# A transformer kernel on one core: the first attention's index branch is projected first, its scores and choice of keys lie between the later projections

## What is computed

```python
mod = c_act @ w_ada[layer] + b_ada[layer]          # 6 x 1024 modulation values
u = modulate(rmsnorm(h, attn_gain[layer]), a_shift, a_scale)
q, k, v, iq, ik, iw = split(u @ w_in)              # 1024, 256, 256, 512, 64, 8 columns
q, k, iq, ik = apply_rope(each)
iw = iw * (IDX_HEADS ** -0.5 * IDX_DIM ** -0.5)
rel = relu(einsum('bqhd,bsd->bqhs', iq, ik))       # 8 index heads, one index key
# index = sum over heads of iw * rel, causal; the 64 best keys of each query are kept
s = einsum(q, k) * HEAD_DIM ** -0.5                # 16 heads, 4 key heads
p = masked_softmax(s, chosen keys)
h = h + a_gate * ((p @ v) @ w_out)
```

## Time and profile before

| | us |
|---|---|
| median of three runs | 2263.2 |
| lowest, highest | 2262.22, 2263.34 |
| span of the profiled execution, first to last instruction | 2254.8 |
| projections, from the first to the last (span time) | 47.06 to 122.07 |
| index scores and choice of keys | 124.76 to 149.34 |
| attention, up to the output projection | 149.34 to 184.00 |
| first feed-forward matmul | 227.46 |

### The profile page before, as it was taken

How to read it: one execution, slowest core, us unless ns; L and a number is a source line. 1 busy time by engine, 2 the same in 40 slices (tenths; PEclk the granted TensorE clock), 3 DMA queues, 4 the chain that set the end, 5 groups by cost and what they waited for, 6 DMA issues and landing times.

```text
span 2254.8 us, 75616 instructions
## 1 busy us (share of the span) xinstructions
PE 2072.8 (92%) x34420; PEld 1800.9 (80%) x34420; DVE 613.6 (27%) x1472; ACT 409.8 (18%) x820; POOL 11.8 (1%) x20
## 2 busy tenths in 40 slices
PE   5967999999999999999999999999988977899998
PEld 3846888878657899999898989898977666777776
DVE  2577553331453201010101010101025372322222
ACT  2033000020463101111111111111112422211111
POOL 0000000000010000000000000000000000000000
PEclk8979999999899899999999999999999998899999
DMA  9453978653475599999999999999981101399996
GB/s 353 146 187 111 374 281 317 241 187 116 152 270 196 194 395 335 393 342 390 385 396 390 396 389 396 387 396 389 396 326 38 38 1 37 156 405 403 405 399 262
DMA packets 253308, 640.84 MB, mean 284 GB/s; under 512 B 15152, under 2 KB 21424, under 8 KB 247984
## 3 DMA queue, kind: packets, MB, share of 16 engines
q1 hardware_dynamic: 252384, 634.93, 74.9%
q10 hardware_dynamic: 848, 4.84, 0.6%
HBM read 638.68 MB, written 1.05 MB: 284 GB/s over the span
## 4 chain that ended last, share of the span: by engine, by line
PE 68%; DMA 20%; DVE 6%; ACT 2%; SPq 2%; issue 1%; DVEq 0%; POOLq 0%; POOL 0%; ACTq 0%
PE psum L745 22%; DMA ring<-in_moe_w_up 13%; PE psum L503 9%; DMA ring<-in_w_up 6%; PE psum L645 3%; PE psum L654 3%; PE psum L630 3%; PE psum L848 3%; PE psum L725 2%; SPq L2275 2%; PE psum L1084 1%; PE psum L839 1%; PE psum L1234 1%; PE psum L798 1%; PE psum L463 1%; PE psum L513 1%
## 5 line engine op out<-in xcount | busy, mean ns | idle before, releaser
L745 PE MATMUL psum<-uT,ring 128*64 128x80 f32 (+1 forms) x14336 | 564.5, 237 | 24.1 <-DMA ring<-in_moe_w_up 21.8
L745 PEld LDWEIGHTS psum<-uT,ring 128*64 128x64 f32 x14336 | 532.5, 137 | 54.2 <-DMA ring<-in_moe_w_up 37.6
L745 PE MATMUL psum<-arena,ring 128*64 128x80 f32 (+1 forms) x7168 | 269.4, 236 | 0.0
L745 PEld LDWEIGHTS psum<-arena,ring 128*64 128x64 f32 x7168 | 263.8, 137 | 0.0
L1755 DVE TENSOR_TENSOR arena<-arena,psum 128x288 f32<-128x288 f32 x56 | 25.4, 454 | 730.6 <-PE psum L745 730.6
L1385 ACT ACTIVATE arena<-psum 128x384 f32<-128x384 f32 x56 | 27.4, 490 | 697.9 <-PE psum L745 697.9
L1608 DVE SCALAR_TENSOR_TENSOR arena<-ring,cact,arena 128x512 f32<-128x512 f32 x168 | 126.3, 752 | 6.0
L503 PE MATMUL psum<-uT,ring 128*128 128x256 f32 (+1 forms) x496 | 111.0, 384 | 3.6 <-ACT uT L1290 3.6
L503 PEld LDWEIGHTS psum<-uT,ring 128*128 128x128 f32 (+1 forms) x496 | 94.2, 191 | 22.0 <-issue 8.3
L503 PE MATMUL psum<-arena,ring 128*128 128x256 f32 x384 | 86.2, 386 | 4.9 <-ACT arena L1290 3.6
L645 PE MATMUL psum<-uT,ring 128*128 128x256 f32 x352 | 80.1, 387 | 10.4 <-DMA ring<-in_ffn_w_gate 10.4
(11 more groups left out here) (417 smaller groups left out, 2081.2 us busy)
## 6 DMA issues: line engine op xcount, KB each, us to landing
ring<-in_moe_w_gate SPq DMA_DIRECT2D x224, 512.0 KB, 11.1
ring<-in_moe_w_up SPq DMA_DIRECT2D x224, 512.0 KB, 10.1
ring<-in_moe_w_down SPq DMA_DIRECT2D x224, 512.0 KB, 11.1
ring<-in_w_ada SPq DMA_DIRECT2D x36, 2048.0 KB, 14.3
ring<-in_w_up SPq DMA_DIRECT2D x19, 2048.0 KB, 11.2
ring<-in_w_down SPq DMA_DIRECT2D x19, 2048.0 KB, 9.9
ring<-in_w_gate SPq DMA_DIRECT2D x19, 2048.0 KB, 10.5
ring<-in_ffn_w_gate SPq DMA_DIRECT2D x5, 2048.0 KB, 7.8
```

The costliest lines, as they stand in the source:

```text
L745: mm = pe.matmul(out(HD * hc), w[:, c0 + HD * hc:c0 + HD * hc + HD], x, skip_group_check=True, **kw)
```

## The change

The index branch comes first. Chunks are loaded in the order `win.3`, `win.4`, `win.0`, `ada0.4`, `ada0.5`, `win.1`, `win.2`, `ada0.6`. The 16 index scores are split into groups of four, six and six behind the query projections, their relus and sums likewise, and the two choices of keys lie between the sums and the rotary steps on VectorE. Keys and v are projected last. The weighing of `ada0.6` is cut into its eight blocks, one behind the maximum of each attention unit, and the column sums of `ada0.4` to `ada0.6` go into the attention on TensorE. The arithmetic is the same.

```diff
-        for n, (c0, c1) in enumerate(((0, 512), (512, 1024), (1024, 1536), (1536, 2048), (2048, 2120))):
-            add_cols(f"win.{n}", w_in, c0, c1)
-        for c in range(FIRST, 7):
+        def add_win(n):
+            add_cols(f"win.{n}", w_in, 512 * n, min(512 * n + 512, w_in.shape[1]))
+        add_win(3)
+        add_win(4)
+        add_win(0)
+        for c in range(FIRST, 6):
             add_cols(f"ada0.{c}", A["w_ada"][0], 512 * c, 512 * c + 512)
+        add_win(1)
+        add_win(2)
+        add_cols("ada0.6", A["w_ada"][0], 512 * 6, 512 * 6 + 512)
...
+            def index_scores(i0, i1):
+                pe.wait_ge(s_rope, 3)
+                for i in range(i0, i1):
+                    t, h = i // IDX_H, i % IDX_H
+                    L, r = P * (t + 1), (h % 2) * HD
+                    b, _ = open_job(pe, "I", "A")
+                    pe.matmul(b[:, 0:L], iqT[r:r + HD, h // 2, P * t:P * t + P], ikd[r:r + HD, 0:L],
+                              start=True, stop=True).then_inc(res, 1)
+            w = chunk("win.3")
             proj("raw", "A", w, 0, 2, uT, base=0)
             proj("raw", "A", w, 256, 2, uT)
+            frees("win.3")
+            rope_unit("pair", 0)
+            w = chunk("win.4")
+            proj("raw", "A", w, 0, 1, uT, rows=HD)
+            rope_unit("pair", 1)
+            tokproj("iw", "V", w, 64, 8, uT)
+            frees("win.4")
+            w = chunk("win.0")
+            proj("raw", "A", w, 0, 2, uT)
+            rope_unit("one", 2)
+            proj("raw", "A", w, 256, 2, uT)
             frees("win.0")
-            rope_unit("pair", 0)
+            rope_unit("pair", 3)
+            index_scores(0, 4)
             w = chunk("win.1")
             proj("raw", "A", w, 0, 2, uT)
-            rope_unit("pair", 1)
+            rope_unit("pair", 4)
+            index_scores(4, 10)
             proj("raw", "A", w, 256, 2, uT)
             frees("win.1")
-            rope_unit("pair", 2)
+            rope_unit("pair", 5)
+            index_scores(10, 16)
             w = chunk("win.2")
             proj("raw", "A", w, 0, 2, uT)
-            rope_unit("pair", 3)
+            rope_unit("pair", 6)
+            rope_unit("dup", 7)
             tokproj("v", "A", w, 256, 256, uT)
...
+            def first_sums(s):
+                if s in (2, 3):
+                    column_sums(s - 1, acc0(s + 2), 4 * (s + 2))
+                if s == len(att_units("dsa")):
+                    column_sums(3, acc0(6), 24)
...
             attention("dsa", [lambda r, g, L: kd[r:r + HD, 0, g, 0:L]],
-                      [lambda w, j, g: vt[0:w, 0, j, HD * g:HD * g + HD]])
+                      [lambda w, j, g: vt[0:w, 0, j, HD * g:HD * g + HD]], first_sums)
...
+            raws(0)
+            raws(1)
+            raws(2, rows=HD, n=1)
+            raws(3)
+            raws(4)
+            index_relu(0, 4)
+            raws(5)
+            index_relu(4, 10)
+            raws(6)
+            index_relu(10, 16)
+            raws(7)
+            copy_job("v", vt[:, 0], lambda b: b3(b, 2))
             attention("dsa")
...
                     if s < len(units):
                         scored(s)
+                    if kind == "dsa" and s < KT:
+                        weigh_block("ada0.6", acc0(6), s)
                     if s >= 2:
                         combine(s - 2)
...
+            V(rope_pair(iqT[:, 0:2, :], raw[:, 0], mark["raw"][0]), s_rope)
+            weigh("ada0.4", acc0(4))
+            V(rope_pair(iqT[:, 2:4, :], raw[:, 1], mark["raw"][1]), s_rope)
+            b = next_job(dve, "iw", "V")
+            V(ts(iw[:], b[:, 0:16].rearrange("p (t n) -> p t n", t=2), IDX_H ** -0.5 * HD ** -0.5, None, ALU.mult), dve_took)
+            weigh("ada0.5", acc0(5))
+            V(rope_dup(b3(ikd, 1), ("dup0", "rotdup0"), 1), s_rope)
+            V(rope_pair(qT[:, 0:2, :], raw[:, 1], mark["raw"][3]), s_rope)
+            index_sums(0, 4)
+            V(rope_pair(qT[:, 2:4, :], raw[:, 0], mark["raw"][4]), s_rope)
+            index_sums(4, 8)
+            best_keys(0)
+            index_sums(8, 10)
+            V(rope_pair(qT[:, 4:6, :], raw[:, 1], mark["raw"][5]), s_rope)
+            index_sums(10, 16)
+            best_keys(1)
+            V(rope_pair(qT[:, 6:8, :], raw[:, 0], mark["raw"][6]), s_rope)
+            V(rope_dup(kd[:, 0, 0:2, :]))
+            V(rope_dup(kd[:, 0, 2:4, :]), s_rope)
             attention("dsa", [selm])
```

More of the change, by code:

```diff
@@ L891, in _ @@
             mm.then_inc(res, 1)
-            w = chunk("win.0")
+            def index_scores(i0, i1):
[6 more added lines that the diff above has]
+                              start=True, stop=True).then_inc(res, 1)
@@ L905, in _ @@
             proj("raw", "A", w, 0, 2, uT)
-            rope_unit("pair", 3)
+            rope_unit("pair", 6)
+            rope_unit("dup", 7)
             tokproj("v", "A", w, 256, 256, uT)
             frees("win.2")
[L909 to L923, removed]
-            pe.wait_ge(s_rope, 8)
[L925 to L931, removed]
+            def first_sums(s):
[3 more added lines that the diff above has]
+                    column_sums(3, acc0(6), 24)
@@ L1419, in _, with index_relu @@
             act.activation(trig[:], ang[:, 0:2, :], ACT.Sin).then_inc(s_trig, 1)
[L1420 to L1428, removed]
+            def index_relu(i0, i1):
+                for i in range(i0, i1):
+                    L = P * (i // IDX_H + 1)
                     b = next_job(act, "I", "A")
-                    i = IDX_H * t + h
                     if i >= 2:
@@ L1599, in mods_from, with weigh_block @@
                 V(stt(m, o, float(D), bias.rearrange("p (a b) -> p a b", b=1).to_broadcast([P, w // rep, rep]), ALU.mult, ALU.add), s_mod)
-            def weigh(name, acc):
[L1603 to L1608, removed]
+            def weigh_block(name, acc, k):
+                slot, val, a, b = place[name]
+                w = slot_view(slot, a, b)
+                if k == 0:
+                    dve.wait_ge(land[slot], val)
+                    V(ts(acc, w[:, 0, :], cact[:, 0:1], None, ALU.mult))
+                else:
+                    V(stt(acc, w[:, k, :], cact[:, k:k + 1], acc, ALU.mult, ALU.add), s_acc if k == KT - 1 else None)
+            def weigh(name, acc):
+                for k in range(KT):
+                    weigh_block(name, acc, k)
             def gain(dst, scale, g):
@@ L1937, in _, with index_sums @@
             dve.wait_ge(s_trig, 1)
-            for i in range(4):
-                V(rope_pair(qT[:, 2 * i:2 * i + 2, :], raw[:, i % 2], mark["raw"][i]), s_rope)
-                if i % 2:
-                    weigh(f"ada0.{4 + i // 2}", acc0(4 + i // 2))
-            V(rope_dup(kd[:, 0, 0:2, :]))
-            V(rope_dup(kd[:, 0, 2:4, :]), s_rope)
-            weigh("ada0.6", acc0(6))
-            V(rope_pair(iqT[:, 0:2, :], raw[:, 1], mark["raw"][5]), s_rope)
-            V(rope_pair(iqT[:, 2:4, :], raw[:, 0], mark["raw"][6]), s_rope)
-            b = next_job(dve, "iw", "V")
-            V(ts(iw[:], b[:, 0:16].rearrange("p (t n) -> p t n", t=2), IDX_H ** -0.5 * HD ** -0.5, None, ALU.mult), dve_took)
-            V(rope_dup(b3(ikd, 1), ("dup0", "rotdup0"), 1), s_rope)
             causal = pk("causal", NT)
-            for t in range(NT):
-                L = P * (t + 1)
-                for h in range(IDX_H):
-                    i = IDX_H * t + h
+            def index_sums(i0, i1):
+                for i in range(i0, i1):
+                    t, h = i // IDX_H, i % IDX_H
+                    L = P * (t + 1)
                     dve.wait_ge(*mark["I"][i])
@@ L1961, in _, with best_keys @@
                         V(stt(acc8[:, 0:L], rel[:, i % 2, 0:L], w, acc8[:, 0:L], ALU.mult, ALU.add), s_relused)
+            def best_keys(t):
+                L = P * (t + 1)
                 V(tt(work[:, 0:L], acc8[:, 0:L], causal[:, t, 0:L], ALU.add))
```

## The result

| | before | changed |
|---|---|---|
| median (range) of 4 runs each, us | 2262.71 (2261.66 to 2263.34) | 2246.75 (2244.59 to 2251.13) |
| ratio, 95% interval | | 0.9933 [0.992, 0.9945] |
| span of the profiled execution, us | 2254.8 | 2244.6 |
| first masked score, us from the span's start | 149.34 | 135.88 |
| output projection, us | 184.00 | 170.18 |

The account below looks back on a forecast made before the run. It took the choice of keys, exposed with TensorE nearly unused, as what to hide; −17.9 + 1.2 + 1.7 + 1.0 = −14.0 gave a span of 2240.8 us and a time of 2249.2 us, range 2244.8 to 2253.6.

Parts of the forecast that it names:

- The bound: Ahead of attention, the choice of keys costs 24.5 us with TensorE nearly unused.
- The walk: New order stepped through up to attention: first masked score at 131.5 instead of 149.34, 17.9 us earlier.
- The rule that what stands ahead in an engine's list is finished first: On VectorE, the 9.1 us choice ahead of the last query pair's rotary holds v back.
- The alternative without that rule: VectorE free to take the last rotary first: v would start at 120.5, the sum would be −16.5.
- The clock behind iw, +1.7: Wide projection behind iw's narrow matmuls: 3.4 us at half speed, 1.7 us lost.
- The clock in v, +1.0: Low clock in v after TensorE's 2.5 us wait: 1.0 us lost, taken between 0 and 1.7.
- Attention, +1.2: Third weighing's eight blocks in attention overfill VectorE's waits: 1.2 us lost, bounds 0 and 6.0.
- Behind it: From the output projection on, order is unaltered and all moves as one piece; first feed-forward matmul stays 43.5 us behind.
- (a): Rival: TensorE is never held and the clock never falls; −19.2, 2244.0 us; chance 0.15.
- (b): Rival: index scores wait for ScalarE's relus and the clock is low in attention; −9.9, 2253.3 us; chance 0.18.
- (c): Rival: the clock stays down after the narrow matmuls, through the projections; +7.9, 2271.1 us; chance 0.02.
- (d): Rival: bank rotation keeps the order from being realised, choice of keys exposed again; gain about 0, 2263 us; chance 0.03.

Follow-up runs that it names:

- scores_last: Changed kernel with all index scores, relus, sums and both choices of keys put back behind v: 2262.3 us, ratio 0.9995 to the kernel before.
- choice_last: Changed kernel with the second choice of keys moved behind the last rotary steps on VectorE: 2250.16 us, ratio 0.9948 to the kernel before.
- iw_merged: Changed kernel with iw computed as eight more rows of the index key's projection, turned back by two small transposes: 2240.18 us, ratio 0.9902 to before.
- split_choice: Changed kernel with the last rotary steps put between four and four rounds of the second choice of keys: 2246.38 us, ratio 0.9926 to before.
- weighed_early: Changed kernel with ada0.6 weighed whole in VectorE's wait behind the index key's rotary, not in attention blocks: 2249.89 us, ratio 0.9945 to before.
- changed_again: The changed kernel itself, unaltered, timed and profiled again beside later variants: 2249.54 us, ratio 0.994 to the kernel before.
- split_and_merged: Changed kernel with the edits of both split_choice and iw_merged: 2236.96 us, ratio 0.9881 to the kernel before.
- filled_wait: Changed kernel with two more matmuls of 512 columns, whose result nobody reads, ahead of v: 2250.12 us, ratio 0.9945 to before.

## Why the prediction was right, point by point

- **The bound.** Right. The exposed choice of keys went beside the projections, and with it the gain comes and goes (scores_last).
- **The walk.** Right to half a us. It gave 98.1 us for the rotation of the second query pair including the clock (96.4 + 1.7), and VectorE took it up at 98.39. The waits came out near what was written: 1.8 foretold at the index scores and 1.61 measured, though the releaser is VectorE's rotary step behind the first choice and not ScalarE's relu; 7.04 and 5.26 us left to VectorE ahead of the projections, where 6 and 5 were foretold. v was to start at 123.0 + 1.7 = 124.7 and did at 124.94, after a wait of 2.19 (2.5 foretold).
- **The rule that what stands ahead in an engine's list is finished first.** It holds for both sides: the choice held the rotary and v (changed), and the rotary's wait held the choice (choice_last). The alternative without that rule, v at 120.5, is out.
- **The clock behind iw, +1.7.** Right: 8.41 us on the chain where the clean projections took 6.91, 1.5 lost. The fall itself came at 71.2, in the last us of iw's matmuls, and lasted to 74.6.
- **The clock in v, +1.0.** Too small, and the first step that was off. I took a value between 0 and 1.7, which was a choice and not worked out; v took 8.88, which is 1.97 over 6.91. Of this 1.7 is the clock, the upper bound (8.86 and 7.17 for v behind the same wait in iw_merged). The rest is that 6.91 is the spacing of projections that follow each other without a wait; behind a wait v takes 7.2 even at full clock. With the 0.24 us by which v starts later, v ends 1.2 us behind the forecast (133.82 and 132.6). Another 0.46 us went missing between v's end and the first masked score: 2.06 us, where the walk had 1.6 (129.9 to 131.5). The walk counted the copy and the first scores alone, which took 0.61 and 0.73 as expected. The chain has two gaps between the engines besides, 0.24 ahead of the scores and 0.43 behind them, in which it shows nothing waited for; split_choice has them too (0.27 and 0.46). In all the first masked score came 13.5 us earlier and not 15.2, so 1.7 us too late.
- **Attention, +1.2.** Too much: 34.30 us where 35.86 was foretold, 0.4 less than before instead of 1.2 more. The blocks cost an estimated 0.7 (weighed_early). The low clock covered 6.8 us of the stage instead of 11.1 before, which I had taken as unchanged; what is left, 34.66 + 0.7 - 34.30 = 1.1, is put down to it by subtraction. The error here (1.6 too much) and the one ahead of it (1.7 too little) cancel, and it is luck that the output projection came at 170.18 for 170.0.
- **Behind it.** The first feed-forward matmul kept its distance, 43.44 us (43.46 before), and TensorE waited for no load before 130 us: "moves as one piece" is right in order, but the clock added 3.6 us in the profiled pair. The predicted shift of −14.0 stands against −16.0 by the first medians and −11.0 by those of changed_again. The two differ by more than either does from the forecast, so a total within 2.4 us says little; the positions in the stage say more.
- **The rivals.** (a), no wait and no loss of clock, didn't happen by itself, but split_and_merged builds it: 160.24, 9.9 us ahead of the changed kernel. That is more than the 5.2 by which (a) undercut the forecast; iw's own 3.7 us, which vanish too, make it 8.9. (b) was wrong in its first half: no relu held TensorE, whose 1.61 us were released by VectorE. Its second half, a low clock in attention, is what the profiles of choice_last and filled_wait show: 3.3 to 3.6 us there. Whether that belongs to the edits or to these executions, which ran 3.2 and 2.3 us over the medians of their kernels, is not shown. That choice_last gains nothing follows without it, since its first masked score stands where it stood. (c) and (d) fell: the clock recovered 3.4 to 6.8 us after its fall behind iw, and the order was realised.

## What to carry to other kernels

Before moving a long piece of work on a strictly ordered engine into another engine's shadow, walk both lists to the first step that one engine frees and the other needs; put that step in the middle of the long piece, since ahead of it or behind it one of the two engines waits. Look for narrow matmuls amid dense ones and merge them into a neighbour's rows: here they cost 3.7 us of their own, and in the profiled executions about as much again behind them (1.4 in the next projection, 1.7 in v, 0.75 in attention). And read a gain from the positions in the first affected stage and from medians over many runs, since two profiled executions differ by several us in stretches that nobody touched.

## What the runs showed of the hardware

- During or at the end of the matmuls of eight columns (32 in the trace), in which TensorE is never idle, the granted clock went from 1.00 to 0.50 in all seven profiles of kernels that have them amid projections, and in neither of the two without. The wide projection behind took 8.5 to 9.7 us in the former and 7.17 in the latter. The kernel before has the same fall behind its iw. For 48 columns it isn't as clear: the fall near 584 us before comes at the end of 32 matmuls of 128x48 (580.23 to 584.03), but in the changed kernel the same matmuls end at 571.65 and the clock stays at 1.00 until 576.4, with a wait of 2.3 us between.
- A wait of 2.2 us ahead of v was followed by a low clock in three of four profiles (v 8.86 us in each); in iw_merged the same 2.18 us was followed by 1.00 and 7.17 us. What differs is the low stretch some 50 us earlier, and that all stands 5.9 us earlier. Whether either decides it was not tried. So the wait alone does not bring the slow v, but in the five profiles with less than 0.5 us of it v was never slow.
- The low clock is not removed for good where one fall is avoided: split_choice, choice_last and filled_wait have a clean v and more low clock in the attention behind it (10.2, 17.1 and 17.1 us, against 6.8), in one profile each, so that a link is not shown. Over the profiles of kernels with the weighing in the attention, the stage takes 33.6 us with 3.4 us of low clock and 37.6 to 38.0 with 17.1, about 0.3 us lost for each us at the lower level; in dense projections it is a half.
